# Low parts of the hidden units from GpSimd to VectorE, and a quarter of the last gate's sum behind the attention

## What is computed

```python
mod = silu(c) @ w_mod + b_mod            # six vectors of 2048: shift1, scale1, gate1, shift2, scale2, gate2
h = rms_norm(x, g_pre_mix) * (1 + scale1) + shift1
q, k, v, q_idx, k_idx, w_idx, pool_in, lru_in, lru_gate = split(h @ w_in)
mixed = concat(rms_norm(top_k_attention(q, k, v, ...)), rms_norm(pool(pool_in)), rms_norm(rglru(lru_in, lru_gate)))
x = x + gate1 * rms_norm(mixed @ w_out, g_post_mix)
h = rms_norm(x, g_pre_mlp) * (1 + scale2) + shift2
u = relu(h @ w_mlp_up)                   # 2048 -> 8192
x = x + gate2 * rms_norm((u * u) @ w_mlp_down, g_post_mlp)
```

## Time and profile before

| | us |
|---|---|
| median of three runs | 2445.08 (2442.55 to 2452.15) |
| the profiled execution | 2449.64 |
| its span, first to last instruction | 2447.8 |
| TensorE busy | 2240.0 (92%) |
| VectorE busy | 1908.7 (78%) |
| ScalarE busy | 976.4 (40%) |
| GpSimd busy | 759.2 (31%) |

### The profile page before, as it was taken

One profiled execution on the slowest core, in us unless ns is written; L12 is line 12 of the kernel. 1 busy time (PEld: TensorE's weight loads), 2 busy tenths in 40 slices (PEclk: granted clock), 3 DMA queues, 4 the chain that ended last, 5 costly groups with the idle time before them and its releaser, 6 DMA issues.

```text
span 2447.8 us, 39446 instructions
## 1 busy us (share of the span) xinstructions
PE 2240.0 (92%) x15364; PEld 1995.7 (82%) x15364; DVE 1908.7 (78%) x1996; ACT 976.4 (40%) x1201; POOL 759.2 (31%) x470
## 2 busy tenths in 40 slices
PE   5998999999899999799888898888979999999996
PEld 1566768887678788798888888888879999999996
DVE  6659975995647665988898888988867787788788
ACT  4333424223246323745444454454433333333342
POOL 6533344444345000044243343433300021212115
PEclk8998999999999999999999999999989999999998
DMA  8976663336633684245444454444853825627424
GB/s 314 363 281 243 240 231 77 107 97 232 215 91 100 183 321 148 84 161 192 150 173 159 163 188 163 163 166 169 313 207 111 337 104 201 248 104 277 172 104 155
DMA packets 180665, 459.14 MB, mean 188 GB/s; under 512 B 17712, under 2 KB 76720, under 8 KB 168368
## 3 DMA queue, kind: packets, MB, share of 16 engines
q1 hardware_dynamic: 117104, 389.60, 44.4%
q10 hardware_dynamic: 63424, 67.64, 8.1%
HBM read 381.42 MB, written 75.51 MB: 187 GB/s over the span
## 4 chain that ended last, share of the span: by engine, by line
PE 25%; DVE 14%; issue 13%; ACT 4%; DMA 2%; ACTq 1%; DVEq 0%; POOL 0%; POOLq 0%
PE psum L1033 8%; PE psum L1031 8%; PE psum L1032 8%; DVE w_lo L2420 3%; ACT w_hi L1749 2%; DVE s_tmp L2436 2%; DMA u2f<-f_lo 2%; ACTq L1829 1%; ACT u_st L1809 1%; DVE unit_odd L2444 1%; DVE w_lo L2451 1%; DVE unit_odd L2438 1%; DVE unit_odd L2441 1%; DVE raw L2441 1%; DVE u_t L2615 1%
## 5 line engine op out<-in xcount | busy, mean ns | idle before, releaser
L928 POOL TENSOR_TENSOR w_lo<-raw,w_hi 128x1024 fp32r<-128x1024 f32 (+1 forms) x96 | 239.0, 2494 | 368.0 <-ACT w_hi L1463 368.0
L1031 PE MATMUL psum<-T_parts,w_hi 128*128 128x256 f32 x1024 | 291.6, 285 | 35.2 <-DVE w_lo L2420 27.7
L1031 PE MATMUL psum<-w_hi,T_parts 128*128 128x256 f32 x1024 | 290.0, 283 | 3.4 <-DVE w_lo L2451 3.4
L1033 PE MATMUL psum<-w_hi,T_parts 128*128 128x256 f32 x1024 | 290.5, 284 | 0.0
L1032 PE MATMUL psum<-T_parts,w_hi 128*128 128x256 f32 x1024 | 288.1, 281 | 0.0
L1033 PE MATMUL psum<-T_parts,w_lo 128*128 128x256 f32 x1024 | 287.9, 281 | 0.0
L1032 PE MATMUL psum<-w_lo,T_parts 128*128 128x256 f32 x1024 | 287.8, 281 | 0.0
L1031 PE MATMUL psum<-B_parts,w_hi 128*128 128x256 f32 x768 | 223.0, 290 | 57.5 <-DVE w_lo L2420 55.2
L1463 ACT ACTIVATE w_hi<-raw 128x1024 fp32r<-128x1024 f32 (+1 forms) x128 | 129.3, 1015 | 354.8 <-PE psum L1033 247.3
L1031 PE MATMUL psum<-h_hi,w_hi 128*128 128x512 f32 (+1 forms) x592 | 239.3, 404 | 14.2 <-issue 9.9
L994 POOL TENSOR_TENSOR y_half<-y_half,part 128x512 f32<-128x512 f32 x44 | 87.2, 1991 | 521.1 <-DVE y_half L2501 521.1
(11 more groups left out here) (357 smaller groups left out, 6332.3 us busy)
## 6 DMA issues: line engine op xcount, KB each, us to landing
raw<-in_w_in SPq DMA_DIRECT2D x88, 512.0 KB, 5.8
mod_ring<-in_w_mod_first SPq DMA_DIRECT2D x32, 1024.0 KB, 8.8
mod_slab<-in_w_mod SPq DMA_DIRECT2D x32, 1024.0 KB, 5.7
raw<-in_w_up_units SPq DMA_DIRECT2D x64, 512.0 KB, 4.4
unit_odd<-in_w_up_units SPq DMA_DIRECT2D x64, 512.0 KB, 5.1
raw<-in_w_down_units SPq DMA_DIRECT2D x64, 512.0 KB, 5.6
unit_odd<-in_w_down_units SPq DMA_DIRECT2D x64, 512.0 KB, 5.3
T_parts<-u2f SPq DMA_DIRECT2D x32, 1024.0 KB, 13.7
```

The costliest lines, as they stand in the source:

```text
L928: nc.gpsimd.tensor_tensor(w_lo[:, s % RING, :, 0:n], raw[:, s % RING, :, 0:n], w_hi[:, s % RING, :, 0:n].bitcast(F32), ALU.subtract).then_ ...
L1031: nc.tensor.matmul(o, a_hi, b_hi, start=first, stop=False)
L1033: return nc.tensor.matmul(o, a_lo, b_hi, start=False, stop=last)
```

## The change

Two things, with new constants `GATE_FIRST = 16` and `GATE_OUT = 8`.

The last 8 of the 32 gate halves are no longer loaded and added in the projections: the loop of SyncE issues halves up to s = 83, VectorE adds 16 before the squares and 8 behind. Halves 24 to 31 are loaded and added in the output groups; the sum over the partitions moves from group 11 behind the third slab of the third output group, the two VectorE steps behind it and the store of the column follow it, and TensorE's wait for `gate_read` moves from ahead of the attention to ahead of the last output group.

In the first MLP matrix `f_lo` moves from GpSimd to VectorE (`form_low`), at m = 4 for the unit before; GpSimd keeps the four sums (T1 ahead of T3 now). `forms_high` moves from m = 3 to m = 2. Unit 2 and the last unit get matching positions.

```diff
-GATE_FIRST = 18
+GATE_FIRST = 16
+GATE_OUT = 8
...
-                if GATE_AT <= s < GATE_AT + GATE_HALVES // 2:
+                if GATE_AT <= s < GATE_AT + (GATE_HALVES - GATE_OUT) // 2:
                     load_gate(2 * (s - GATE_AT))
                     load_gate(2 * (s - GATE_AT) + 1)
...
-                if k == 2:
+                if k == SG - 1:
+                    load_gate(GATE_HALVES - GATE_OUT)
+                    load_gate(GATE_HALVES - GATE_OUT + 1)
+                if k == 3 * SG:
                     sp.wait_ge(gate_col, 2)
                     store_gate(sp, 1)
                 if k == SG:
                     sp.wait_ge(mixed_ready, KD)
+                if SG <= k < SG + GATE_OUT - 2:
+                    load_gate(GATE_HALVES - GATE_OUT + 2 + k - SG)
...
-            def forms(unit, first=False):
+            def form_sums(unit):
                 pool.wait_ge(u_sq_ready, unit + 1)
-                ch.put(nc.gpsimd.tensor_tensor(uf[:, U_T3, :], uf[:, U_B22, :], uf[:, U_B12, :], ALU.subtract))
-                loop_link(nc.gpsimd.tensor_tensor(uf[:, U_T1, :], uf[:, U_B12, :], uf[:, U_B11, :], ALU.subtract), unit, 1)
-                loop_link(nc.gpsimd.tensor_tensor(uf[:, U_T2, :], uf[:, U_B22, :], uf[:, U_T1, :], ALU.subtract), unit, 2)
+                nc.gpsimd.tensor_tensor(uf[:, U_T1, :], uf[:, U_B12, :], uf[:, U_B11, :], ALU.subtract).then_inc(t_summed, 1)
+                nc.gpsimd.tensor_tensor(uf[:, U_T3, :], uf[:, U_B22, :], uf[:, U_B12, :], ALU.subtract).then_inc(t_summed, 1)
+                pool.wait_ge(t_summed, unit * 3 + 2)
+                nc.gpsimd.tensor_tensor(uf[:, U_T2, :], uf[:, U_B22, :], uf[:, U_T1, :], ALU.subtract).then_inc(t_summed, 1)
+                pool.wait_ge(t_summed, unit * 3 + 3)
                 nc.gpsimd.tensor_tensor(uf[:, U_T4, :], uf[:, U_B21, :], uf[:, U_T2, :], ALU.subtract).then_inc(f_formed, 1)
-                pool.wait_ge(f_formed, unit + 1)
-                pool.wait_ge(f_hi_ready, unit + 1)
-                if not first:
-                    pool.wait_ge(f_stored, unit * 32)
-                nc.gpsimd.tensor_tensor(f_lo[:], uf[:, U_B11:, :], f_hi[:].bitcast(F32), ALU.subtract).then_inc(f_lo_ready, 1)
...
-                if j == SG - 2:
-                    pe.wait_ge(gate_step, GATE_HALVES)
-                    for k in range(KD):
-                        last = nc.tensor.matmul(bank(STAGE["g10"], 2)[:, k:k + 1], acc_g[:, P * k:P * k + P], ones[:, 0:1], start=True, stop=True)
-                    last.then_inc(gate_sum, 1)
...
-            pe.wait_ge(gate_read, 1)
...
+            def gate_sums(j):
+                if j == 2:
+                    pe.wait_ge(act_freed, freed("A", STAGE["out1"] + 1))
+                    pe.wait_ge(dve_freed, freed("D", STAGE["out1"] + 1))
+                    pe.wait_ge(gate_step, GATE_HALVES)
+                    for k in range(KD):
+                        last = nc.tensor.matmul(bank(STAGE["out1"], 1)[:, k:k + 1], acc_g[:, P * k:P * k + P], ones[:, 0:1],
+                                                start=True, stop=True)
+                    last.then_inc(gate_sum, 1)
...
+                if d == TT - 1:
+                    pe.wait_ge(gate_read, 1)
...
@@ ScalarE, after_product, unit 2 @@
-                    if m == 0:
+                    if m == 1:
                         forms_high(0, 0)
                     if m == 3:
                         store_forms(0, 0)
+                    if m == 4:
                         finish_unit(1, 0)
-                    if m == 5:
+                    if m == 6:
                         forms_high(1, 0)
...
-                if m == 3:
+                if m == 2:
                     forms_high(n - 1, i)
                 if m == 6:
                     store_forms(n - 1, i)
...
@@ ScalarE, after_down @@
                     if m == 0:
                         finish_unit(BLOCK - 1, UNITS // BLOCK - 1)
+                    if m == 2:
+                        forms_high(BLOCK - 1, UNITS // BLOCK - 1)
                     if m == 3:
-                        forms_high(BLOCK - 1, UNITS // BLOCK - 1)
-                    if m == 5:
                         store_forms(BLOCK - 1, UNITS // BLOCK - 1)
...
@@ VectorE @@
-            for q in range(GATE_FIRST, GATE_HALVES):
+            for q in range(GATE_FIRST, GATE_HALVES - GATE_OUT):
                 gate_add(q)
...
+            def form_low(n, i):
+                unit = i * BLOCK + n
+                dve.wait_ge(f_formed, unit + 1)
+                dve.wait_ge(f_hi_ready, unit + 1)
+                if not at_start(i) or n:
+                    dve.wait_ge(f_stored, unit * 32)
+                V.tensor_tensor(f_lo[:], uf[:, U_B11:, :], f_hi[:].bitcast(F32), ALU.subtract).then_inc(f_lo_ready, 1)
...
@@ VectorE, after_down: after dn_low, ahead of dn_sum @@
+                if isinstance(kb, int) and kb == 0 and n == 0:
+                    if m == 2:
+                        form_low(BLOCK - 1, UNITS // BLOCK - 1)
...
@@ VectorE, output groups, d the group, s the slab @@
+                    if d == 1 and q < GATE_HALVES:
+                        gate_add(q)
+                        q += 1
+                    if s == PROJ_SLABS + 2 * SG + 7:
+                        dve.wait_ge(gate_sum, 1)
+                        V.tensor_tensor(mod[:, 5, :], bank(STAGE["out1"], 1)[:, 0:KD], cols("b_mod5"), ALU.add).then_inc(gate_read, 1)
+                        dve.wait_ge(gate_read, 1)
+                        V.tensor_tensor(mod[:, 5, :], mod[:, 5, :], cols("g_post2"), ALU.mult).then_inc(gate_col, 1)
+                if d == 0:
+                    for q in range(q, q + 2):
+                        gate_add(q)
+                    q += 1
...
@@ VectorE, after_product: behind op_low and weight_sum @@
+                if at_start(i) and n == 2:
+                    if m == 2:
+                        form_low(0, 0)
+                    if m == 6:
+                        form_low(1, 0)
+                    return
+                if m == 4:
+                    form_low(n - 1, i)
```

More of the change, by code:

```diff
@@ L560, in build @@
         stage_done, act_freed, dve_freed = sem("stage_done"), sem("act_freed"), sem("dve_freed")
-        t_chain = sem("t_chain")
+        t_summed = sem("t_summed")
         dve_chain, act_chain, pool_chain = sem("dve_chain"), sem("act_chain"), sem("pool_chain")
@@ L968, in _ @@
                 squares_of(hd)
-            def forms(unit, first=False):
+            def form_sums(unit):
                 pool.wait_ge(u_sq_ready, unit + 1)
-                ch.put(nc.gpsimd.tensor_tensor(uf[:, U_T3, :], uf[:, U_B22, :], uf[:, U_B12, :], ALU.subtract))
-                loop_link(nc.gpsimd.tensor_tensor(uf[:, U_T1, :], uf[:, U_B12, :], uf[:, U_B11, :], ALU.subtract), unit, 1)
-                loop_link(nc.gpsimd.tensor_tensor(uf[:, U_T2, :], uf[:, U_B22, :], uf[:, U_T1, :], ALU.subtract), unit, 2)
-                nc.gpsimd.tensor_tensor(uf[:, U_T4, :], uf[:, U_B21, :], uf[:, U_T2, :], ALU.subtract).then_inc(f_formed, 1)
-                pool.wait_ge(f_formed, unit + 1)
-                pool.wait_ge(f_hi_ready, unit + 1)
-                if not first:
-                    pool.wait_ge(f_stored, unit * 32)
-                nc.gpsimd.tensor_tensor(f_lo[:], uf[:, U_B11:, :], f_hi[:].bitcast(F32), ALU.subtract).then_inc(f_lo_ready, 1)
-            def loop_link(instruction, unit, nth):
-                instruction.then_inc(t_chain, 1)
-                pool.wait_ge(t_chain, unit * 2 + nth)
+                nc.gpsimd.tensor_tensor(uf[:, U_T1, :], uf[:, U_B12, :], uf[:, U_B11, :], ALU.subtract).then_inc(t_summed, 1)
[3 more added lines that the diff above has]
+                pool.wait_ge(t_summed, unit * 3 + 3)
+                nc.gpsimd.tensor_tensor(uf[:, U_T4, :], uf[:, U_B21, :], uf[:, U_T2, :], ALU.subtract).then_inc(f_formed, 1)
             def add_parts(c, kb, last=False):
@@ L994, in add_parts @@
                     nc.gpsimd.tensor_tensor(y, y, part[:], ALU.add).then_inc(y_pool, 1)
-            forms(0, True)
+            form_sums(0)
             with pool.Fori(1, UNITS) as unit:
-                forms(unit)
+                form_sums(unit)
             pool.wait_ge(dn_done, DN_KEYS * DN_EVICTIONS)
@@ L1323, in _ @@
                           ready=mixed_ready if d == 0 else None, tile=out_tile,
-                          after=after_out0 if d == 0 else lambda j: None)
+                          after=(after_out0, lambda j: None, gate_sums)[d])
                     continue
@@ L2321, in _ @@
             head_split(1)
[L2322 to L2325, removed]
             done("g11")
@@ L2532, in x1_scales @@
                 scaled_identity(first, end, 4)
-            g = 4 * KD
+            g, q = 4 * KD, GATE_HALVES - GATE_OUT
             for d in range(TT):
```

## The result

The changed kernel takes 2432.72 us (median of nine runs, 2428.01 to 2437.59), the kernel before 2449.01 (nine runs, 2442.55 to 2454.89): 16.3 us less, a ratio of 0.9939, 95% interval 0.9924 to 0.9955. The profiled span goes from 2447.8 to 2430.9 us, 16.9 less.

The account below looks back on a forecast made before the run. TensorE, busy 92% of the span, was taken as the bound, so gains lie where it stands still. Terms of -11.5, -3.6, -2 and -3 made -20 us; from the median of 2445.08 this gave 2425 us, range 2404 to 2446.

Parts of the forecast that it names:

- Gate, -11.5: Projections: without eight gate halves the norm sums start 9.7 us sooner and, at full clock, take 1.8 less.
- The bound of -13.4: Projections: the most the gate part could gain, with no late slab, -13.4 us.
- The gate sum moved, 0: Third output group: the 32 gate-sum matmuls leave group 11 but stay on TensorE's path, 0 us.
- Output groups, 0: Output groups: added halves hide on VectorE, 4.9 of 5.60 us per slab; 0 taken, at worst +6 us.
- Unit, -0.13: First MLP matrix: `f_lo` on VectorE gains, a new wait for A11 nearly cancels it; -0.13 us per unit, -3.6 in all.
- the first rival: First MLP matrix: A11 is not held up, -1.93 us per unit over 28 units, 2375 us; chance 0.08.
- Start of the matrix, -2: First MLP matrix's start: unit 3's stretched S4 goes, -3.9, and `f_lo` on VectorE adds 1.9; -2 us.
- Boundary, -3: Far end of the first MLP matrix: an earlier last store and TensorE's spare work, -3 us, bounds -6 and +3.
- TensorE's spare product: Far end of that matrix: one product, 2.8 us, left for TensorE during the last store, saving a second wait and clock fall.
- The faster `f_lo`: Far end of that matrix: `f_lo` in 1.95 us instead of some 4 sends the last store some 2 us earlier.
- The sum: Whole kernel: -11.5, -3.6, -2 and -3 make -20 us, predicting 2425 us.
- The second rival: MLP gives nothing, as VectorE and GpSimd exclude each other; only the gate's -11.5 is left, 2434 us; chance 0.22.

Follow-up runs that it names:

- gate_only: The kernel before with only the gate halves' and gate sum's part of the change: 2434.0 us, 0.9941 to the kernel before.
- fhi_m3: The changed kernel with `forms_high` back behind product 3 instead of 2, low parts still on VectorE: 2380.73 us, 0.9723 to the kernel before.
- last_later: The changed kernel with the last unit's high parts, low parts and store two products later in the second matrix's first unit: 2431.46 us in one run.
- low_only: The kernel before with only the forms' part of the change, the gate untouched: 2443.14 us, 0.9969 to the kernel before.
- flo_twice: The changed kernel with every low part of the forms made twice on VectorE: 2502.25 us in one run.
- store_late2: The changed kernel with high parts behind product 4, low parts behind 5, forms' stores moved later, some second-matrix slab loads behind the last store: 2337.88 us, 0.9537.

## Why the prediction was right, and where not

The forecast was the likeliest case and its time lay within the range. Its reading by stages:

- **Gate, -11.5.** -11.3 in after, -11.6 in gate_only. The steps hold: norm sums predicted at 651.0, found at 652.29 with 0.6 of it ahead of the change; slab 85 predicted to go out at 616, found at 617.68; late slabs 1.5 predicted, 1.3 found; full clock at the norm sums. The bound of -13.4 is a slip: 11.2 and 1.8 make 13.0.
- **The gate sum moved, 0.** Right, and the trace shows why it had to be reckoned in both places. In after:

```profile
879.26 3.63 PE L1318 MATMUL psum<-ones,acc_g 128*128 128x1 f32 x32
882.75 0.75 PE L1029 MATMUL psum<-w_hi,m_hi 128*128 128x512 f32 x1
...
886.25 0.40 PE L1031 MATMUL psum<-w_hi,m_lo 128*128 128x512 f32 x1
```

  Nothing waits; but the matmuls behind it start 0.43 us apart, where it is 0.23 at full clock, until 886.25. The third output group takes 49.9 us where it took 44.8: 5.1 more, which group 11 no longer pays for the same sum. The attention starts 15.8 us sooner and the first combine only 11.3.
- **Output groups, 0.** Right: the first two keep their length (46.6 and 44.8 us from the start of one to the next, in both kernels).
- **Unit, -0.13.** -0.14, for the reasons given: `f_lo` 1.95 predicted and 2.02 found, the new wait for A11 1.8 predicted and 1.72 found. fhi_m3 is the first rival made true: it gave 2375 for a kernel in which A11 is not held up, and that kernel takes 2381.
- **Start of the matrix, -2.** Mis-sized: -0.2 (units 2 to 4 take 78.8 us, before 79.0). The stretched S4 of the earlier trace rows is gone, but the wait for A11, which the prediction reckoned with in the loop's units alone, is there too. In after:

```profile
1078.87 1.23 DVE L2421 TENSOR_TENSOR w_lo<-raw,w_hi 128x1024 fp32r<-128x1024 f32 x1 [2.26 <-ACT w_hi L1753]
```

  In fhi_m3, without that wait, the two units that the change reorders take 53.8 us instead of the 55.7 of before and of after: the predicted 2 us.
- **Boundary, -3.** Mis-sized: the last unit is 1.3 us shorter and what follows it 1.1 longer, 0.2 in all. Two steps failed. TensorE's spare product was to save time: its waits there come to 17.4 us, to 17.1 in before, and last_later shows that the place in which VectorE blocks does not move `part`. The faster `f_lo` was to send the last store 2 us earlier. It did shorten the step from `f_hi` to that store, from 6.3 to 4.3 us, but the store then took 13.4 us until `part` and not 12.3, and the store before it went out 0.8 us later behind the last combine but one and took 0.3 longer to land. So `part` comes 68.3 us behind that combine, in before 68.2. ScalarE in before, the last store and `part`:

```profile
1784.71 0.59 ACTq L1829 DMA_DIRECT2D u2f<-f_lo  x1
...
1796.99 0.60 ACT L1892 ACTIVATE part<-psum 128x512 f32<-128x512 f32 x1 [10.54 <-DMA u2f<-f_lo]
```

- **The sum.** -20 predicted, -16.3 measured, -16.9 in the spans. The two ends fell short by 4.6 us. That the spans miss by only 3.1 is luck: the one long unit of before, worth 1.9 us, is in no term. The rest of the distance from 2425 to 2432.7 is the kernel before: its first three runs had a median of 2445.08, nine have 2449.01.
- The second rival (nothing from the MLP, 2434) gave nearly the same time as was measured, by another mechanism; low_only and fhi_m3 tell them apart.

## What to carry to other kernels

When an operation moves to another engine, ask in what place of every in-order queue its producer and its store now stand: here the move itself was worth 53 us, and one position of `f_hi` on ScalarE hid nearly all of it. Follow the loop through the queues from the operation that ends it back to itself; each time the last wait in it goes, look again, until the bounding engine has none left. An operation that waits for something late, a store above all, belongs behind those that wait for nothing.

## What the runs showed of the hardware

- 32 matmuls of one column cost their 3.63 us and then some 1.5 us more: TensorE's granted clock is 0.83 from 880 to 890 us in after, though no wait stands there; before, the same loss lay behind group 11 (0.83 from 700 to 710).
- In flo_twice the mean granted clock from 1100 to 1600 us is 0.90, in after it is 0.97 (1100 to 1700), in store_late2 1.00; TensorE is busy 437 and 500 of 500 us in the first and the last. The busy share alone does not tell: gate_only is busy 439 us and keeps 1.00. Its longest single wait there is 1.6 us, in after 2.4, in flo_twice 4.0. Behind a wait of 2.22 us in after, matmuls that stood 0.12 us apart come 0.21 apart, and the clock is 0.66 from 1530 to 1535. The unit of flo_twice is still only as long as the added work makes it.
- The same store of 1792 columns lands 6.2 us after its issue in the loop of after (DMA share 0.49 from 1100 to 1700) and 27 us after it between the matrices (1.02 to 1.04 from 1730 to 1770).
- GpSimd's sum of 256 columns takes 0.75 us and 1.60 in one unit of after (1513.08 and 1514.60), the longer ones while VectorE makes low parts from SBUF; the combine beside the first, which reads PSUM, takes 0.42 (1513.10).
